# Prompt attention: probabilities and v as pairs of rounded parts, row sums on GpSimd, and an earlier first load for the streams

## The reference, cut to what matters

```python
def fox_block(qi, cq, qpos, k, v, ck):
    scale = FOX_DIM ** -0.5
    logits = jnp.einsum('bqhd,bkhd->bhqk', qi, k, preferred_element_type=jnp.float32) * scale
    logits = logits + cq[..., :, None] - ck[..., None, :]
    mask = jnp.arange(k.shape[1])[None, :] <= qpos[:, None]
    logits = jnp.where(mask, logits, -jnp.inf)
    p = jax.nn.softmax(logits, axis=-1).astype(v.dtype)
    return jnp.einsum('bhqk,bkhd->bqhd', p, v)
...
    qkv = jax.nn.silu(causal_dwconv(hist, gdn_conv_w))
...
    o_gdn, new_gdn_state = gdn_chunked(qd, kd, vd, g, beta, gdn_state.astype(f32), min(CHUNK, T))
...
    h = x + jnp.einsum('bte,ed->btd', mix, w_o)
```

## Time and profile before

| | us |
|---|---|
| median of 3 runs (3948.92 to 3954.96) | 3954.55 |
| the profiled execution's own time | 3959.77 |
| its span | 3958.1 |
| the prompt's part of the stage `heads`, about 780 to 1780 | 1000 |
| the streams' part, with the last delta chunks, about 1780 to 2098 | 318 |

### The profile page before, as it was taken

One profiled execution on the slowest core, in us unless ns is written; L12 is line 12 of the kernel. 1 busy time (PEld: TensorE's weight loads), 2 busy tenths in 40 slices (PEclk: granted clock), 3 DMA queues, 4 the chain that ended last, 5 costly groups with the idle time before them and its releaser, 6 DMA issues. The chain is left out here.

```text
span 3958.1 us, 55054 instructions
## 1 busy us (share of the span) xinstructions
PE 3749.1 (95%) x20957; PEld 3247.4 (82%) x20957; DVE 1625.0 (41%) x3498; ACT 1195.4 (30%) x2333; POOL 332.6 (8%) x407
## 2 busy tenths in 40 slices
PE   7999999699999999999998979999999999899998
PEld 7999999577777777676676869999999999688886
DVE  4000477555544554444433434444444444432222
ACT  4112222233333333332212323333333333221111
POOL 3100000211211211111100000000000000000000
PEclk9999999799999999999989989999999999899999
DMA  4221222401221122015433431111111111342222
GB/s 149 69 68 63 62 69 67 90 23 40 54 49 39 34 49 45 18 53 170 143 116 107 128 85 47 44 46 44 46 44 44 46 44 46 106 153 80 81 80 67
DMA packets 346870, 277.73 MB, mean 70 GB/s; under 512 B 117554, under 2 KB 312482, under 8 KB 346615
## 3 DMA queue, kind: packets, MB, share of 16 engines
q1 hardware_dynamic: 333007, 256.13, 22.0%
q0 software_dynamic: 5040, 18.09, 1.3%
q10 hardware_dynamic: 8652, 1.14, 0.3%
HBM read 189.65 MB, written 85.65 MB: 70 GB/s over the span
## 5 line engine op out<-in xcount | busy, mean ns | idle before, releaser
L2415 PE MATMUL bank<-hn_hi,up_w_parts 128*128 128x436 f32 (+1 forms) x3520 | 981.8, 360 | 10.1 <-DVE up_w_parts L2490 10.1
L2415 PEld LDWEIGHTS bank<-hn_hi,up_w_parts 128*128 128x128 f32 x3520 | 662.1, 188 | 42.1 <-issue 10.2
L2415 PE MATMUL bank<-hn_lo,up_w_parts 128*128 128x436 f32 (+1 forms) x1760 | 632.9, 360 | 0.0
L2415 PEld LDWEIGHTS bank<-hn_lo,up_w_parts 128*128 128x128 f32 x1760 | 331.4, 188 | 19.2
L332 PE MATMUL bank<-proj_wh,proj_xh 128*128 128x256 f32 (+1 forms) x1088 | 309.5, 285 | 0.0
L332 PE MATMUL bank<-proj_wl,proj_xh 128*128 128x256 f32 (+1 forms) x1088 | 306.7, 282 | 0.0
L332 PE MATMUL bank<-proj_wh,proj_xl 128*128 128x256 f32 (+1 forms) x1088 | 306.6, 282 | 0.0
L2461 ACT COPY up_raw<-bank 128x436 f32<-128x436 f32 (+1 forms) x220 | 110.3, 502 | 642.3 <-PE bank L2415 612.3
L1436 PE MATMUL bank<-heads_p_pT,heads_p_v 128*65 128x512 f32 (+3 forms) x640 | 289.4, 534 | 10.7 <-issue 10.1
L2486 DVE TENSOR_SCALAR up_hist<-up_raw 128x2 f32 (+2 forms) x264 | 44.9, 170 | 551.3 <-ACT up_acc L2465 547.6
L2655 PE MATMUL bank<-down_w_hi,down_g_hi 128*128 (+1 forms) x748 | 231.5, 391 | 14.4 <-DVE down_g_lo L2719 14.4
(11 more groups left out here) (413 smaller groups left out, 6792.0 us busy)
## 6 DMA issues: line engine op xcount, KB each, us to landing
up_w<-in_w_up_dram SPq DMA_DIRECT2D x44, 512.0 KB, 4.8
down_g_raw<-scratch_g SPq DMA_DIRECT2D x110, 192.0 KB, 2.3
scratch_g<-up_acc SPq DMA_DIRECT2D x88, 218.0 KB, 2.0
heads_s_k<-in_cache_fox_k_dram SPq DMA_DIRECT2D x8, 2048.0 KB, 13.3
heads_s_v<-in_cache_fox_v_dram SPq DMA_DIRECT2D x8, 2048.0 KB, 8.3
heads_d_qkvT<-scratch_gch SPq DMA_DIRECT2D x17, 768.0 KB, 5.6
down_y<-in_w_down_dram SPq DMA_DIRECT2D x22, 512.0 KB, 3.6
scratch_gch<-proj_work SPq DMA_DIRECT2D x48, 218.0 KB, 1.9
```

The source lines that it names most:

```text
L2415: mm = pe.matmul(bank[:, pair(n) + e, 0:width], w_parts[:, a, part, e, k, :], x[:, k, cols], start=(k == 0 and m == 0), stop=(k == KD - 1 ...
```

## The change

Prompt's second product is made from rounded parts. `v` is split once per head into `v_parts` (64 columns hi, 64 columns lo; an ACT copy and a DVE subtraction). ACT takes each block's exponential twice, once rounded into `p_hi` and once in full into `p`; DVE writes `p_lo = p - p_hi`. PE multiplies `p_lo` with v's hi part and `p_hi` with both parts at once (128 output rows), both in fp32r. At a group's end ACT copies rows 64 to 127 to `oT_rest` and DVE adds rows 0 to 63. The ones column is gone: GpSimd adds every block's `p` into `total`, and four small float32 matmuls with a column of ones per group give the sums (`turn_out`). The tiles of exponentials have two buffers instead of three. GpSimd's list is now woven from Delta's and Prompt's. The plan's constants change, `v` is staged in the first half of `ktok`, and the streams' first two key loads are issued under the last head, where `k[0]` and `k[1]` both lie over tiles of the even heads.

```diff
-    PERIOD = 72.0
+    PERIOD = 68.0
...
-    SPEED = 0.62
+
+    SPEED = 0.6
...
+        self.v = self.ktok[:, :, 0:FD]
+        self.v_parts = ph.sb("p_v_parts", [P, 2, NB, 2 * FD], F32R)
+        self.p = ph.sb("p_p", [P, 2, BANK])
+        self.p_hi, self.p_lo = ph.sb("p_p_hi", [P, 2, BANK], F32R), ph.sb("p_p_lo", [P, 2, BANK], F32R)
+        self.total = ph.sb("p_total", [P, 2, BANK])
...
-            return 2.65e-3 * sum(self.width(G, b) for b in range(self.blocks(G))) + 0.95e-3 * first + 1.6 + \
+            return 1.9e-3 * sum(self.width(G, b) for b in range(self.blocks(G))) + 0.95e-3 * first + 2.3 + \
...
+            sp.wait_ge(s["row_mm"], self.use["k", h, 3] + 1)
+            sp.dma_start(self.v, io["v_p"][:, h * FD:(h + 1) * FD].rearrange(in_head, p=P)).then_inc(s["v_loaded"], 16)
...
         def turn_out(r, G):
             pe.wait_ge(s["oT_ready"], G + 1)
+            pe.wait_ge(s["total_ready"], self.first_key[G] + self.blocks(G))
+            out = self.row_bank(r)[:, 0:4 * (FD + 1)].rearrange("p (n d) -> p n d", d=FD + 1)
             for i in range(4):
-                mm = pe.transpose(self.row_bank(r)[:, i * (FD + 1):(i + 1) * (FD + 1)], self.oT[:, i * P:(i + 1) * P],
-                                  c["ident"][0:FD + 1, 0:FD + 1])
+                pe.transpose(out[:, i, 0:FD], self.oT[:, i * P:(i + 1) * P], c["ident"][0:FD, 0:FD])
+            for i in range(4):
+                mm = pe.matmul(out[:, i, FD:FD + 1], self.total[:, G % 2, i * P:(i + 1) * P], c["ones"][:, 0:1],
+                               start=True, stop=True)
             mm.then_inc(s["row_mm"], 1)
...
-            yield at + 4.0
+            yield at + (4.0 if b else 5.8)
             if b == 0:
-                pe.wait_ge(s[f"v_loaded{h % 2}"], 16 * (h // 2) + 16)
+                pe.wait_ge(s["v_lo"], h + 1)
                 after(pe, s["oT_ready"], G)
-            pe.wait_ge(s["p_ready"], u + 1)
-            pe.matmul(self.bank[0:self.FD + 1, self.out, BANK - wide:BANK], self.v[:, h % 2, b, :],
-                      self.pT[:, u % 3, BANK - wide:BANK], start=(b == 0), stop=(b == last)).then_inc(s["pv_mm"], 1)
+            pe.wait_ge(s["lo_ready"], u + 1)
+            cols = slice(BANK - wide, BANK)
+            out, v = self.bank[:, self.out, cols], self.v_parts[:, h % 2, b, :]
+            if b == 0:
+                pe.matmul(out, v, self.p_hi[:, u % 2, cols], start=True, stop=False)
+            mm = pe.matmul(out[0:self.FD], v[:, 0:self.FD], self.p_lo[:, u % 2, cols], start=False, stop=False)
+            if b > 0:
+                mm = pe.matmul(out, v, self.p_hi[:, u % 2, cols], start=False, stop=(b == last))
+            mm.then_inc(s["pv_mm"], 1)
...
-            u, wide = self.first_key[G] + b, self.width(G, b)
+            u, cols = self.first_key[G] + b, slice(BANK - self.width(G, b), BANK)
+            logits = self.bank[:, self.keys[u % 2], cols]
             yield at + 1.6
             act.wait_ge(s["key_mm"], u + 1)
-            after(act, s["pv_mm"], u - 2)
-            nc.scalar.activation(self.pT[:, u % 3, BANK - wide:BANK], self.bank[:, self.keys[u % 2], BANK - wide:BANK],
-                                 ACT.Exp).then_inc(s["p_ready"], 1)
+            after(act, s["pv_mm"], u - 1)
+            nc.scalar.activation(self.p_hi[:, u % 2, cols], logits, ACT.Exp)
+            after(act, s["lo_ready"], u - 1)
+            after(act, s["total_ready"], u - 1)
+            nc.scalar.activation(self.p[:, u % 2, cols], logits, ACT.Exp).then_inc(s["p_ready"], 1)
+
+    def v_due(self, h):
+        return self.group_at[(h - 1) * self.NG + 3] if h else 26.0
+
+    def v_scalar(self, act):
+        s, nc, FD = self.s, self.nc, self.FD
+        for h in range(self.FH):
+            yield self.v_due(h)
+            act.wait_ge(s["v_loaded"], 16 * h + 16)
+            if h >= 2:
+                act.wait_ge(s["pv_mm"], self.first_key[(h - 1) * self.NG])
+            nc.scalar.copy(self.v_parts[:, h % 2, :, 0:FD], self.v).then_inc(s["v_hi"], 1)
...
             act.wait_ge(s["pv_mm"], self.first_key[G] + self.blocks(G))
+            after(act, s["oT_ready"], G)
+            nc.scalar.copy(self.oT_rest[:], self.bank[self.FD:2 * self.FD, self.out, :]).then_inc(s["oT_rest_ready"], 1)
+
+    def gpsimd(self, pool):
+        s, nc = self.s, self.nc
+        for (G, b), at in self.key_at.items():
+            u, cols = self.first_key[G] + b, slice(BANK - self.width(G, b), BANK)
+            total, p = self.total[:, G % 2, cols], self.p[:, u % 2, cols]
+            yield at + 2.8
+            pool.wait_ge(s["p_ready"], u + 1)
+            if b == 0:
+                if G >= 2:
+                    pool.wait_ge(s["row_mm"], self.use["o", G - 2] + 1)
+                ins = nc.gpsimd.tensor_copy(total, p)
+            else:
+                pool.wait_ge(s["total_ready"], u)
+                ins = nc.gpsimd.tensor_tensor(total, total, p, ALU.add)
+            ins.then_inc(s["total_ready"], 1)
+
+    def keys_vector(self, dve):
+        s, nc = self.s, self.nc
+        for (G, b), at in self.key_at.items():
+            u, cols = self.first_key[G] + b, slice(BANK - self.width(G, b), BANK)
+            yield at + 2.8
+            dve.wait_ge(s["p_ready"], u + 1)
+            after(dve, s["pv_mm"], u - 1)
+            nc.vector.tensor_tensor(self.p_lo[:, u % 2, cols], self.p[:, u % 2, cols],
+                                    self.p_hi[:, u % 2, cols].bitcast(F32), ALU.subtract).then_inc(s["lo_ready"], 1)
+
+    def v_vector(self, dve):
+        s, nc, FD = self.s, self.nc, self.FD
+        for h in range(self.FH):
+            yield self.v_due(h) + 1.2
+            dve.wait_ge(s["v_hi"], h + 1)
+            nc.vector.tensor_tensor(self.v_parts[:, h % 2, :, FD:], self.v,
+                                    self.v_parts[:, h % 2, :, 0:FD].bitcast(F32), ALU.subtract).then_inc(s["v_lo"], 1)
+
+    def out_vector(self, dve):
+        s, nc = self.s, self.nc
+        for G in range(self.groups):
+            yield self.key_at[G, self.blocks(G) - 1] + 5.9
+            dve.wait_ge(s["oT_rest_ready"], G + 1)
             if G >= 1:
-                act.wait_ge(s["row_mm"], self.use["o", G - 1] + 1)
-            nc.scalar.copy(self.oT[:], self.bank[0:self.FD + 1, self.out, :]).then_inc(s["oT_ready"], 1)
+                dve.wait_ge(s["row_mm"], self.use["o", G - 1] + 1)
+            nc.vector.tensor_tensor(self.oT[:], self.bank[0:self.FD, self.out, :], self.oT_rest[:], ALU.add) \
+                .then_inc(s["oT_ready"], 1)
...
-        yield self.prompt.end - 30.0
+        last_head = (self.prompt.FH - 1) * self.prompt.NG
+        yield self.prompt.group_at[last_head + 2]
+        sp.wait_ge(self.prompt.s["pv_mm"], self.prompt.first_key[last_head + 1])
         load_k(0)
+        load_k(1)
...
-            d.gpsimd(pool)
+            weave(d.gpsimd(pool), p.gpsimd(pool))
...
-            weave(d.vector(dve), p.vector(dve), t.vector(dve))
+            weave(d.vector(dve), p.vector(dve), p.keys_vector(dve), p.v_vector(dve), p.out_vector(dve), t.vector(dve))
...
```

103 lines of the change are left out of this document (57 added, 46 removed).

## The result

| | before | after |
|---|---|---|
| median, us (4 runs each) | 3954.76 (3948.92 to 3957.48) | 4041.64 (4039.63 to 4054.21) |
| ratio to before, 95% interval | | 1.0228 [1.0205, 1.0252] |
| span of the profiled execution, us | 3958.1 | 4039.9 |
| mean granted TensorE clock of the span | 0.976 | 0.961 |

A forecast was written before the change was run, and what follows sets the result against it. TensorE's list was taken as the bound. Work -67, last quarters +24, VectorE's lateness +25, other waits +5 and early load -1 gave -14 us: likeliest median 3940, forecast's own range 3920 to 3947, 8-in-10 range 3895 to 4000.

The forecast's parts named there:

- TensorE's work falls by 95 - 28 = 67 us, between 56 and 86.: TensorE: the fp32r product saves 95 us, the one-column matmuls at the groups' ends cost 28.
- Some 0.7 of a chunk moves behind the prompt ... I count it at zero.: Plan constants: some delta work moves from the prompt's stretch to the streams', not saved, counted at zero.
- I take 3 us each, 24 in all: Last quarter of each head: subtraction and addition take turns, 35 us against TensorE's 33; loss 24 us in all.
- the pair's throughput: Last quarters: a block's subtraction and addition run one after the other, 1.97 us a block, about 35 us a quarter.
- I take 25 us, a third: Other quarters: subtractions blocked by GpSimd make VectorE's list late for TensorE; 25 us of at most 77.
- 5 us more: ScalarE's doubled exponentials and two buffers instead of three add a little to TensorE's waits: 5 us.
- The rival: Outside the last quarters VectorE's list becomes the bound: all 77 us blocked, +38 us, 3992; border 39 us; chance 0.35.
- there is next to no clock to win in the first stretch: Prompt's stretch: TensorE's granted clock is already 0.99 of full speed; no term in the sum.
- The early load: Start of the streams' part: issuing the first two key loads earlier gains at most 2 us, counted as 1.
- What would show it: Signs in the changed profile: matmul distance, subtraction length, TensorE's busy time; idle growth over 67 us in the prompt means slower.

The follow-up runs named there:

- run 12: The changed kernel without the four one-column matmuls at each group's end, additions wide: 4010.67 us, 1.0138 of the kernel before.
- run 1: The changed kernel with GpSimd's additions cut to one column, sums then wrong: 3985.42 us, 1.0073 of the kernel before.
- run 9: The changed kernel with GpSimd's additions and VectorE's subtraction both cut to one column: 3954.37 us, 0.9996 of the kernel before.
- run 11: The changed kernel with three one-pass products, sums from a ones column beside v's upper part, nothing on GpSimd: 3975.57 us, 1.0054 of the kernel before.
- run 7: The kernel before with only the streams' first keys loaded under the last head and tiles split for it: 3958.08 us, 1.0006.
- run 8: The kernel before with exponentials and v rounded once to fp32r and one product of 65 columns: 3839.10 us, 0.9710 of the kernel before.
- run 4: The changed kernel with four buffers and the product planned 2.0 us later, the transposition reading oT only 0.4 us: 4039.89 us, 1.0211.
- run 13: The changed kernel without the one-column matmuls and with GpSimd's additions one column wide: 3962.86 us, 1.0017 of the kernel before.

## Why the prediction was wrong

The sum had -67 for work, +53 for idle time (24 + 25 + 5 - 1) and nothing for the clock. Measured are -52, +78 and +54. Two steps failed: the clock had no term at all, and the idle time was priced by blocked subtractions, with 5 us for everything else. The steps one by one:

- *"TensorE's work falls by 95 - 28 = 67 us, between 56 and 86."* 52 us. The one-column matmuls cost 29.6 us (28 predicted), by the work that run 12 saves, 0.92 us a group. The product saved the rest, 52 + 30 = 82, just under the lowest of the 84 to 106 that were predicted.
- *"Some 0.7 of a chunk moves behind the prompt ... I count it at zero."* Right as work: 20 us of it moved (3000 to 2844 of delta's matmul records in the prompt's part, 0.7 of a chunk) and the streams' part grew by 24.5 us. Without it the prompt's part would have shown its loss more plainly: 72 us less work there, and the part is 56 us longer.
- *"I take 3 us each, 24 in all"* for the last quarters. The size comes near, the mechanism doesn't hold. The eight last quarters of each kernel (sum of eight windows, from one group's result to the next's), after, and with narrow additions:

```profile
sum 298.72, PE 265.50 PEld 222.35 DVE 207.84 ACT 159.98 POOL 198.50; mean PE 33.19 PEld 27.79 DVE 25.98 ACT 20.00 POOL 24.81
```

```profile
sum 271.17, PE 250.60 PEld 212.19 DVE 178.71 ACT 159.33 POOL 90.89; mean PE 31.32 PEld 26.52 DVE 22.34 ACT 19.92 POOL 11.36
```

  A last quarter lasts 37.3 us as before (298.8 / 8 in the earlier trace rows; 36 predicted), all its saving spent: 31.0 us of work, 4.2 idle and 2.2 lost at half clock. The prediction had it bound by the pair's throughput, with the subtraction or GpSimd at work for 35 us of it. In the trace one or the other is at work for 28.1 of the 37.3 us. So the pair was not the bound; it made TensorE wait at single blocks. Without the additions' width a last quarter takes 33.9 us: 27.5 us for eight, half of what the width costs, 12.6 of it idle time and 14 clock.
- *"I take 25 us, a third"* and *"5 us more"*: one of the two steps that failed. Idle time grew by 78 us: 24 in the last quarters (298.72 - 265.50 = 33.2, against 298.8 - 290.0 in the earlier trace rows), 46 in the rest of the prompt's part and 7 in the streams', against 30 predicted outside the last quarters. The rival had the place right (VectorE's list in order) and put its border at 39 us of lateness. But blocking isn't what was priced too low. Outside the last quarters the 129 full subtractions lost 22 us to it (863.6 ns in the mean against 690), where the prediction took 77 as its bound; and run 1 takes only 14 us of idle time off there (97.6 to 83.9). The other 33 us of the 46 remain with narrow additions, and the 5 us stood for them. Run 9 shows the largest part: with the subtraction's own 0.7 us out of VectorE's list 20 of the 33 go, and 31 us of the kernel's time. I had priced the blocking and put no price on the operation itself.
- *"there is next to no clock to win in the first stretch"*: true, and the wrong question; this is the other step that failed, and the larger. There was clock to lose. 54 us of the 87 are half-clock time that no term held; even the rival's 77 us of lateness gave only 3992. Runs 1, 11 and 12 show that it comes and goes with the change's own parts: 136.5 us at half clock, 71.7 with narrow additions, 85.3 without the one-column matmuls, 20.5 without either. The falls went from 4 to 28.
- *The Trainium skill's rule* on shared reading ("SBUF — State Buffer", section "Who interferes with whom") is borne out in both directions here: the subtraction 887 ns in the mean where it took 716 beside narrow additions, and 1.82 us at most; the addition 1460 ns in the mean where 1276 was the length alone.
- *The early load:* -1 predicted, +0.06% with its interval around zero measured (run 7).
- *What would show it:* the product's two matmuls start 0.23 us apart in a stream (1390.47, 1390.70; 0.24 predicted); the subtraction's mean is 887 ns in full blocks and 795 over all forms (over 900 predicted), its longest 1.82 us (over 1.5 predicted). TensorE's idle time in the prompt's part grew by 70.8 us, over the 67 that I had named as the border. Its busy time in the stage, which was to fall by 56 to 86 us, rose by 2.5 us (1236.0 to 1238.5): the work fell, and the lower clock filled it up.

The sum as measured: -52 work, +78 idle, +54 clock, and 7 outside these parts or between executions, is +87. Against the predicted -14 the miss is 101 us: 15 in the work, 25 in the idle time, 54 in the clock and the 7. What makes the idle time that even run 9 keeps over before's (76.2 against 60.0), and how much of the change's loss two buffers and the product's place make, stays open.

## What to carry to other kernels

Work taken off the bounding engine is worth its full amount only while the engines behind it stay early; price an operation that is put into another engine's ordered list by its own length as well as by its blocking, and expect part of a pure saving (a fifth in run 8) to come back as idle time. Price the clock with the idle time: here 78 us of added gaps came with 54 us lost at half clock, though each gap was short. In this kernel sums that ride in a spare column of a product were cheaper than sums on an idle-looking engine that shares its reading with the one everybody waits for (run 11, 66 us). When you move an operation in the plan to give it slack, move what reads its result as well (run 4).

## What was unexpected about the hardware

The mean granted clock of the prompt's part went from 0.99 to 0.93, though no gap of TensorE was longer than 3.0 us, and the loss (54 us) is of the size of the idle time added (78). Four float32 matmuls with one moving column take as long as the four of L832 with 128 columns in the earlier trace rows: eight records that span 1.05 us, in both. Leaving them out took 51 us of half-clock time away, though the idle time grew by 20. Of the 28 falls 7 stood right behind them, with 0.3 to 1.2 us idle; the other 21 stood behind 1.2 to 2.9 us idle. Without them and with narrow additions 58 us at half clock remain (run 13).
